# Head norm of the last mixer: the four tiles of squares are added on VectorE before one product with ones

## The chip, the cores and the metric

One core of one Trainium2 chip runs the whole program. The metric is the device time of one execution in microseconds, as the median of three runs. A profile is one further execution; its times are read from its trace.

## The reference

Two transformer blocks run over 256 tokens of width 2048, in fp32. The first has three attention branches and a convolutional feed-forward part. The second has an attention mixer over 272 tokens (16 of them meta tokens) and then a gated linear attention (GLA) mixer. The change lies in the end of the GLA mixer:

```
o = (o_f + o_b).transpose(0, 2, 1, 3)[:, pad:]            # per token: 4 heads x 512 values
o = rmsnorm_2(o, o_norm).reshape(B, L, GLA_VALUE_DIM)     # x * rsqrt(mean(x*x) + eps) * w, over the 512 values of a head
return (o * jax.nn.silu(g_out[:, pad:])) @ w_out
```

## The kernel before

**Weights.** Every weight matrix is streamed in units of 128x1024 fp32 (two k tiles by 512 columns). SyncE loads a unit into `raw`, ScalarE copies it to `whi` (rounded for a fast product, L655) and VectorE makes the rest `wlo = raw - whi` (L1304). TensorE multiplies each unit in three passes, (whi, ahi), (whi, alo), (wlo, ahi): 24 products of 128x256 a unit in the stage of this case (L2078). `whi` and `wlo` are rings of four units; ScalarE and VectorE work `LEAD = 3` units ahead of TensorE. ScalarE may start the split of unit u+3 only when TensorE has finished unit u-1 (`ring_waits`).

**The stage `gg`.** The gate projection of the GLA mixer is 4 trips of 8 units, its outputs go through Silu to `gg`. Beside these units, each engine runs the GLA of the four heads. Head h begins at unit `HEAD_AT[h] = 8 * h`, and `head_step(h, lag)` says what an engine does for head h at `lag` units after that. Each engine has its own program in which a step's order is written out by hand:

- TensorE: first the 24 products of the unit, then `head_step` of all heads.
- ScalarE and VectorE, in `trip`: first the split of the unit three ahead, then the read-out of finished banks (at the eighth unit of a trip), and then `head_step` of all heads.

**One head.** TensorE makes the scores at lag 0 and 1 (L2565, L2573), and the head's output of 512 values by 256 tokens at lag 3, in banks 6 and 7, as four tiles `v` of 128x256 (L2617, L2618; `o3_ready`). At lag 3 ScalarE squares them in two instructions into `osq3` (L1236; `o3_sq`) and loads the table of Sqrt (L700). At lag 4 TensorE multiplies the four tiles of squares with a 128x128 matrix of ones, into one bank, which sums over the 512 values and leaves the sum on all partitions (L2624; `o3_sum`); ScalarE takes the root (L1241; `o3_root`) and VectorE the reciprocal (L1978; `o3_rstd`). At lag 5 VectorE scales the four tiles, from the banks (L1982; `o3_scaled`). At unit 8h+7 (`GATED_AT`) VectorE multiplies with `gg` (L2005; `z3_ready`). The next head's scores wait for `o3_root` at its lag 0, and its far scores for `o3_scaled` at its lag 1. VectorE also has for the next head, at its lag -2 (lag 6 of this head), the products of L1950 and L1922.

**The rest.** Stage `gout` multiplies with `w_out`, reads the banks with `gainrow` (L2018), and the last residual is added. The DMA of `gainrow` is issued by ScalarE at lag 3 of the last head (L1232) and counted on its own semaphore `gain_in`. In the trace the tiles `osq3`, `gqk` and `v3` appear as `osq`, `gqk` and `v`.

Of the kernel before, what the change touches and what calls it, by code (L numbers as in the profile page):

```python
# [19 lines left out]
ALU = mybir.AluOpType  # L20
# [6 lines left out]
TB = 256  # L27
# [100 lines left out]
def two_blocks_kernel(nc, A, out):  # L128

    ctx = ExitStack()  # L130
    with ctx:
# [30 lines left out]
        ones = sb("ones", [P, P])  # L162
# [98 lines left out]
        gainrow = sb("gainrow", [P, D], F32, at_=R2 + KD * T2 * 4 + 4 * 2 * D)  # L261
# [4 lines left out]
        bank = ctx.enter_context(nc.psum_tensor("bank", [P, 8, 512], F32))  # L266
# [60 lines left out]
        def unit_source(ph, i, j):  # L327
# [70 lines left out]
        x_parked, x_back, up_clear, gla_const, z_sum, z_abs, z_min, z_exp, z_ln, z_sub, cum_ready, v3_turned, v3_taken = map(  # L398
            sem, "x_parked x_back up_clear gla_const z_sum z_abs z_min z_exp z_ln z_sub cum_ready v3_turned v3_taken".split())
# [2 lines left out]
                sem, "e_q e_k e_d e_dec d_sub q_dec k_inv k_end k_far sc_sum x_sum xm_sum sc_part sc_own sc_ready scm_ready "  # L402
                     "o3_ready o3_sq o3_sum o3_root o3_rstd o3_scaled z3_ready z3hi".split())

        gain_in, out_made, stored = map(sem, "gain_in out_made stored".split())


        LO, lo_tiles = {}, 0
# [236 lines left out]
        def _(act):  # L645
# [561 lines left out]
            def head_step(h, lag):  # L1207

                lf, lb = decays(h)
                if lag == -6:  # L1210
                    for d, t in enumerate((kendf, kendb)):
                        act.wait_ge(d_sub, 3 * h + 2 + d)
                        act.activation(t[:, :, :], t[:, :, :], ACT.Exp, scale=SC).then_inc(e_d, 1)
                    if h:
                        act.wait_ge(sc_sum, 2 * h)
                    for d, l in enumerate((lf, lb)):
                        act.activation(kinv[:, d, :, :], l[:, :, 0:TB], ACT.Exp, scale=-SC).then_inc(e_k, 1)
                if lag == -5:
                    if h:
                        act.wait_ge(x_sum, h)  # L1220
                    for d, l in enumerate((lf, lb)):
                        act.activation(qdec[:, d, :, :], l[:, :, 0:TB], ACT.Exp, scale=SC).then_inc(e_q, 1)
                    act.activation(dec[:, 0, :, :], lf[:, :, GL_CHUNK - 1:TB:GL_CHUNK], ACT.Exp, scale=SC).then_inc(e_dec, 1)
                    act.activation(dec[:, 1, :, :], lb[:, :, 0:TB:GL_CHUNK], ACT.Exp, scale=SC).then_inc(e_dec, 1)
                if lag == 1:
                    act.wait_ge(xm_sum, h + 1)
                    act.activation(scm[0:TM, :], bank[0:TM, 6, 0:TB], ACT.Copy)
                    act.activation(scm[32:32 + TM, :], bank[0:TM, 6, 0:TB], ACT.Copy).then_inc(scm_ready, 1)
                if lag == 3:
                    act.wait_ge(o3_ready, h + 1)  # L1230
                    if h == GL_HEADS - 1:
                        act.dma_start(gainrow[:, :], gain_all).then_inc(gain_in, 16)  # L1232
                    if h:
                        act.wait_ge(z3_ready, h)
                    for c in range(2):
                        act.activation(osq3[:, 2 * c:2 * c + 2, :], bank[:, 6 + c, :].rearrange("p (v t) -> p v t", v=2),  # L1236
                                       ACT.Square).then_inc(o3_sq, 1)
                    load_table(4 + 2 * h, ACT.Sqrt)
                if lag == 4:
                    act.wait_ge(o3_sum, h + 1)  # L1240
                    act.activation(msq[:, 0:TB], bank[:, 4, 0:TB], ACT.Sqrt, bias=eps, scale=1.0 / GL_V).then_inc(o3_root, 1)  # L1241
# [51 lines left out]
        def _(dve):  # L1293
# [649 lines left out]
            def head_step(h, lag):  # L1943

                if lag == -6:
                    to_ends(h)
                if lag == -2:
                    for d in range(2):
                        dve.wait_ge(e_q, 2 * h + d + 1)
                        dve.tensor_tensor(qdec[:, d, :, :], qdec[:, d, :, :], gqk[:, 2 * h:2 * h + 2, 0:TB], ALU.mult)\  # L1950
                           .then_inc(q_dec, 1)
                    far_keys(h)
                flat = sc[:, :, :].rearrange("p s t -> p (s t)")
                if lag == 0:
                    if h:
                        dve.wait_ge(o3_ready, h)
                    own = blocks(flat, 0, P, 0, TB + P, P)
                    other = tmp[:, 0, 0:TB].rearrange("p (t c) -> p t c", t=2)
                    for d, (dst, mask) in enumerate(((own, maskf), (other, maskb))):
                        dve.wait_ge(sc_sum, 2 * h + 2)  # L1960
                        dve.tensor_tensor(dst, bank[:, 4, d * TB:(d + 1) * TB].rearrange("p (t c) -> p t c", t=2),
                                          blocks(mask[:, :], 0, P, 0, 0, P), ALU.mult).then_inc(sc_part, 1)
                    dve.wait_ge(sc_part, 2 * h + 2)
                    dve.tensor_tensor(own, own, other, ALU.add).then_inc(sc_own, 1)
                if lag == 1:
                    dve.wait_ge(sc_own, h + 1)
                    dve.wait_ge(x_sum, h + 1)
                    dve.tensor_copy(flat[:, P:P + TB], bank[:, 5, 0:TB]).then_inc(sc_ready, 1)
                    dve.tensor_copy(blocks(flat, 0, 64, GL_CHUNK, TB + P, GL_CHUNK),
                                    bank[0:64, 5, TB:TB + P].rearrange("p (t c) -> p t c", t=2)).then_inc(sc_ready, 1)  # L1970
                    dve.tensor_copy(blocks(flat, 64, P, 0, TB + P, GL_CHUNK),
                                    bank[64:P, 5, TB:TB + P].rearrange("p (t c) -> p t c", t=2)).then_inc(sc_ready, 1)
                    dve.wait_ge(scm_ready, h + 1)
                    dve.tensor_tensor(scm[64:64 + TM, :], bank[0:TM, 6, 0:TB], scm[0:TM, :].bitcast(F32), ALU.subtract)\
                       .then_inc(scm_low, 1)
                if lag == 4:
                    dve.wait_ge(o3_root, h + 1)
                    dve.reciprocal(rstd[:, 0:TB], msq[:, 0:TB]).then_inc(o3_rstd, 1)  # L1978
                if lag == 5:
                    dve.wait_ge(o3_rstd, h + 1)  # L1980
                    for v in range(4):
                        dve.scalar_tensor_tensor(osq3[:, v, :], bank[:, 6 + v // 2, (v % 2) * TB:(v % 2 + 1) * TB],  # L1982
                                                 column("gla_o_norm_2", v), rstd[:, 0:TB], ALU.mult, ALU.mult)\
                           .then_inc(o3_scaled, 1)
# [25 lines left out]
            def rows_out(i, chunk, u, n):  # L2010

                if 2 * i + chunk == 0:
                    dve.wait_ge(gain_in, 16)
                for tt in range(2):

                    dve.wait_ge(y_squared, 24 + 2 * (2 * i + chunk) + tt + 1)
                    c = 512 * (2 * i + chunk)
                    dve.tensor_tensor(yrow[:, tt, c:c + 512], bank[:, 2 * chunk + tt, :], gainrow[:, c:c + 512], ALU.mult)\  # L2018
                       .then_inc(y_gained, 1)

            stream("gout", rows_out)

            for tt in range(2):
# [16 lines left out]
        def _(pe):  # L2040
# [561 lines left out]
            def head_step(h, lag):  # L2602

                if lag == 0:
                    scores(h)
                if lag == 1:
                    far_scores(h)
                if lag == 3:
                    pe.wait_ge(v3_taken, 3 * TRIPS["gv"])
                    pe.wait_ge(sc_ready, 3 * h + 3)  # L2610
                    pe.wait_ge(scm_low, h + 1)
                    pe.wait_ge(v_low, 2 + GL_HEADS)
                    for v in range(4):
                        col = h * GL_V + v * P
                        o = bank[:, 6 + v // 2, (v % 2) * TB:(v % 2 + 1) * TB]
                        for k in range(2):
                            pe.matmul(o, v3[:, k, col:col + P], sc[:, k, :], start=k == 0, stop=False)  # L2617
                        mm = pe.matmul(o, v3m[0:64 + TM, col:col + P], scm[0:64 + TM, :], start=False, stop=True)  # L2618
                    mm.then_inc(o3_ready, 1)
                if lag == 4:  # L2620
                    pe.wait_ge(sc_part, 2 * h + 2)
                    for v in range(4):
                        pe.wait_ge(o3_sq, 2 * h + v // 2 + 1)
                        mm = pe.matmul(bank[:, 4, 0:TB], ones[:, :], osq3[:, v, :], start=v == 0, stop=v == 3)  # L2624
                    mm.then_inc(o3_sum, 1)

            for i in range(TRIPS["gg"]):
                for j in range(UNITS["gg"]):
# [99 lines left out]
```

## Time and profile before

| | |
|---|---|
| median of 3 runs | 2286.8 us (2285.84 to 2286.86) |
| the profiled execution | 2286.57 us, its span 2284.8 us |
| TensorE busy | 2259.1 us, 99% |
| VectorE busy | 1435.2 us, 63% |
| ScalarE busy | 1172.5 us, 51% |
| stage `gg` | from about 2052 to 2186 us of the span |

The span is the time from the first to the last instruction in the trace; the execution's own time lies 1.8 us above it. TensorE's rows carry modelled ends: neighbouring products overlap on paper, so a unit's cost is read from the starts. A row of busy time by stretch gives the stretch and its length in us, the busy time (and number of instructions) of PE, PEld, DVE, ACT and POOL, the granted clock of TensorE, the DMA engines' share and GB/s.

### The profile page before, as it was taken

The page shows a single profiled execution, that of the slowest core. Times are in us where ns is not written, and L with a number is a line of the kernel's source. Part 1 is how long each engine was busy: PE and PEld are TensorE (multiplying, and loading weights), DVE is VectorE, ACT ScalarE, POOL GpSimd, SP SyncE. Part 2 cuts the span into 40 slices and gives each one's busy share as a digit, 9 for nine tenths or more (in the row PEclk, how much of TensorE's full clock was granted, in tenths as well). Part 3 has the DMA queues.
Part 4 walks back from the last instruction along what each step waited for, and adds up shares of the span by engine and source line. Part 5 has one row for each costly group of instructions (what it writes and reads, how often), then busy time and mean ns, then how long its engine had stood idle before and what let it go on. Part 6 is the DMA issues. An engine that isn't in the chain of part 4 may idle for free.

```text
span 2284.8 us, 43650 instructions
## 1 busy us (share of the span) xinstructions
PE 2259.1 (99%) x17147; PEld 2139.8 (94%) x17147; DVE 1435.2 (63%) x1843; ACT 1172.5 (51%) x1743; POOL 192.3 (8%) x146
## 2 busy tenths in 40 slices
PE   9999999999999999999999999999999999999998
PEld 9898999999899999999988889999999999999986
DVE  5556644458577777777744447997665464566654
ACT  5455544444454554554544445455555455675553
POOL 0000000000001222212200000221000000012110
PEclk9999999999999999999999999999999999999999
DMA  8545566656546656566665564555335556554453
GB/s 290 183 139 157 165 191 195 193 168 236 192 144 210 189 180 209 182 197 199 196 207 187 188 192 143 189 185 164 111 111 186 173 158 186 161 155 123 139 192 139
DMA packets 258873, 405.69 MB, mean 178 GB/s; under 512 B 16656, under 2 KB 115853, under 8 KB 257709
## 3 DMA queue, kind: packets, MB, share of 16 engines
q1 hardware_dynamic: 257060, 396.87, 55.2%
q10 hardware_dynamic: 1688, 7.07, 0.9%
q8 instruction: 89, 1.46, 0.3%
q14 instruction: 36, 0.29, 0.0%
HBM read 396.32 MB, written 4.22 MB: 175 GB/s over the span
## 4 chain that ended last, share of the span: by engine, by line
PE 95%; DVE 2%; ACT 2%; issue 0%; DMA 0%; ACTq 0%; DVEq 0%; SPq 0%
PE bank L2078 67%; PE bank L2183 14%; PE bank L2651 4%; PE bank L2093 2%; PE bank L2397 1%; PE bank L2432 1%; PE bank L2617 1%; PE bank L2573 1%; PE bank L2118 1%; ACT whi L655 0%; PE bank L2369 0%; DVE wlo L1304 0%; PE bank L2406 0%; DMA xtok<-in_x 0%; PE bank L2377 0%
## 5 line engine op out<-in xcount | busy, mean ns | idle before, releaser
L1304 DVE TENSOR_TENSOR wlo<-raw,whi 128x1024 fp32r<-128x1024 f32 (+1 forms) x748 | 927.9, 1250 | 697.3 <-ACT whi L655 694.0
L2078 PE MATMUL bank<-ahi,whi 128*128 128x256 f32 (+1 forms) x4224 | 1196.1, 283 | 3.4 <-DVE alo L1490 1.3
L2078 PE MATMUL bank<-ahi,wlo 128*128 128x256 f32 (+1 forms) x4224 | 1181.4, 280 | 0.0
L2078 PE MATMUL bank<-alo,whi 128*128 128x256 f32 (+1 forms) x4224 | 1181.4, 280 | 0.0
L655 ACT ACTIVATE whi<-raw 128x1024 fp32r<-128x1024 f32 (+1 forms) x748 | 774.7, 1040 | 714.7 <-PE bank L2078 476.8
L2078 PEld LDWEIGHTS bank<-ahi,whi 128*128 128x128 f32 x4224 | 794.2, 188 | 10.7 <-issue 5.3
L2078 PEld LDWEIGHTS bank<-alo,whi 128*128 128x128 f32 x4224 | 794.3, 188 | 1.4 <-issue 0.2
L2078 PEld LDWEIGHTS bank<-ahi,wlo 128*128 128x128 f32 x4224 | 794.4, 188 | 0.0
L2183 PE MATMUL bank<-whi,ghi 128*128 128x512 f32 x352 | 137.0, 389 | 0.0
L2183 PE MATMUL bank<-whi,glo 128*128 128x512 f32 x352 | 136.9, 389 | 0.0
L2183 PE MATMUL bank<-wlo,ghi 128*128 128x512 f32 x352 | 136.9, 389 | 0.0
L2669 POOL CAST ghi<-pr 128x256 f32 x44 | 40.0, 909 | 753.1 <-DVE pr L1701 753.1
L1694 DVE SCALAR_TENSOR_TENSOR cv<-bank,par,cv 128x255 f32<-128x255 f32 (+1 forms) x176 | 78.7, 478 | 11.9 <-DVE cv L1694 1.5
L2183 PEld LDWEIGHTS bank<-wlo,ghi 128*128 128x128 f32 x352 | 66.1, 188 | 13.8
L2183 PEld LDWEIGHTS bank<-whi,glo 128*128 128x128 f32 x352 | 66.1, 188 | 13.7
L2183 PEld LDWEIGHTS bank<-whi,ghi 128*128 128x128 f32 x352 | 66.1, 188 | 13.7 <-DVE wlo L1304 0.2
L2662 POOL TENSOR_TENSOR glo<-pr,ghi 128x256 f32 x44 | 65.8, 1494 | 7.2 <-POOL ghi L2669 7.2
L993 ACT ACTIVATE cv<-bank,par 128x256 f32<-128x256 f32 x88 | 42.5, 564 | 38.4 <-DVE bank L1688 38.4
L2078 PE MATMUL bank<-yhi,wlo 128*128 128x256 f32 x192 | 53.0, 276 | 0.0
L2078 PE MATMUL bank<-yhi,whi 128*128 128x256 f32 x192 | 53.0, 276 | 0.0
L2078 PE MATMUL bank<-ylo,whi 128*128 128x256 f32 x192 | 53.0, 276 | 0.0
L2679 POOL TENSOR_TENSOR nc<-n,cos 128x272 f32<-128x272 f32 x24 | 40.5, 1687 | 120.7 <-DVE n L1722 120.7
(357 smaller groups left out, 2192.8 us busy)
## 6 DMA issues: line engine op xcount, KB each, us to landing
raw<-in_w_up SPq DMA_DIRECT2D x176, 512.0 KB, 4.7
raw<-in_w_in SPq DMA_DIRECT2D x156, 512.0 KB, 4.2
raw<-in_attn_w_in SPq DMA_DIRECT2D x96, 512.0 KB, 4.1
raw<-in_gla_w_in SPq DMA_DIRECT2D x96, 512.0 KB, 3.7
raw<-in_w_down SPq DMA_DIRECT2D x80, 512.0 KB, 4.3
raw<-in_w_out SPq DMA_DIRECT2D x32, 512.0 KB, 4.5
raw<-in_attn_w_out SPq DMA_DIRECT2D x32, 512.0 KB, 3.7
raw<-in_gla_w_out SPq DMA_DIRECT2D x32, 512.0 KB, 4.2
```

The source lines that it names most:

```text
L655: act.activation(whi[:, u % RING, 0:c], raw[:, u % RAW, 0:c], ACT.Copy).then_inc(whi_ready, 1)
L993: act.activation(cv[:, t, :], bank[:, 4 * chunk + t, 0:TB], ACT.Identity, bias=par[:, bass.ds(i * 4 + (PAR["conv_b"] + r), 1)], scale=par[ ...
L1304: dve.tensor_tensor(wlo[:, u % RING, 0:c], raw[:, u % RAW, 0:c], whi[:, u % RING, 0:c].bitcast(F32), ALU.subtract).then_inc(wlo_ready, 1)
L1694: dve.scalar_tensor_tensor(cv[:, t, back:TB], bank[:, 4 * chunk + t, 0:TB - back], tap, cv[:, t, back:TB], ALU.mult, ALU.add).then_inc((ta ...
L2078: mm = pe.matmul(bank[:, base + t, 0:T], w[wp][:, k, col:col + P], rhs(ap, k0 + k), start=begins and k == 0 and (wp, ap) == (0, 0), stop=e ...
L2093: mm = pe.matmul(bank[:, first_bank + tt, 0:cols[1] - cols[0]], ha((ahi, alo)[ap], k0 + k, tt * P, P), w[wp][:, k, cols[0]:cols[1]], start ...
L2118: mm = pe.transpose(turned(k)[:, tt * P:(tt + 1) * P], src[:, tt, k * P:(k + 1) * P], ident[:, :])
L2183: mm = pe.matmul(bank[:, row_bank(b, c, tt), :], tokens_of, w[wp][:, k, :], start=begins and k == 0 and (wp, ap) == (0, 0), stop=ends and ...
L2651: mm = pe.matmul(bank[:, b, :], gated(ap, k0 + k)[:, tt * P:(tt + 1) * P], w[wp][:, k, :], start=begins and k == 0 and (wp, ap) == (0, 0), ...
L2662: pool.tensor_tensor(dst, whole, high.bitcast(F32), ALU.subtract).then_inc(done, 1)
L2669: pool.tensor_copy(ghi[:, bass.ds(i * 4 + t, 1), :], pr[:, t % 2:t % 2 + 1, :]).then_inc(ffhi_ready, 1)
L2679: pool.tensor_tensor(nc2[:, n % 2, :], n2[:, n % 2, :], cos[:, :], ALU.mult).then_inc(qk_cos, 1)
```

## The change

VectorE gets two additions at lag 4, in place in `osq3`: tiles 2 and 3 onto tiles 0 and 1 (128x512), and then tile 1 onto tile 0 (128x256). TensorE then makes one product with the ones where it made four. It waits for the second addition (`o3_added`) where it waited for ScalarE's squares (`o3_sq`). VectorE's reciprocal goes from lag 4 to lag 5, and its four scalings from lag 5 to lag 6. The semaphore `gain_in` goes: the DMA of `gainrow` counts on `gla_const`, which stands at 80 by then and reaches 96.

```
 # ScalarE, head_step, lag 3
                     if h == GL_HEADS - 1:
-                        act.dma_start(gainrow[:, :], gain_all).then_inc(gain_in, 16)
+                        act.dma_start(gainrow[:, :], gain_all).then_inc(gla_const, 16)
 # VectorE, head_step
                 if lag == 4:
+                    dve.wait_ge(o3_sq, 2 * h + 2)
+                    dve.tensor_tensor(osq3[:, 0:2, :], osq3[:, 0:2, :], osq3[:, 2:4, :], ALU.add).then_inc(o3_added, 1)
+                    dve.wait_ge(o3_added, 2 * h + 1)
+                    dve.tensor_tensor(osq3[:, 0, :], osq3[:, 0, :], osq3[:, 1, :], ALU.add).then_inc(o3_added, 1)
+                if lag == 5:
                     dve.wait_ge(o3_root, h + 1)
                     dve.reciprocal(rstd[:, 0:TB], msq[:, 0:TB]).then_inc(o3_rstd, 1)
-                if lag == 5:
+                if lag == 6:
                     dve.wait_ge(o3_rstd, h + 1)
                     for v in range(4):
                         dve.scalar_tensor_tensor(osq3[:, v, :], bank[:, 6 + v // 2, (v % 2) * TB:(v % 2 + 1) * TB],
 # VectorE, rows_out
-                    dve.wait_ge(gain_in, 16)
+                    dve.wait_ge(gla_const, 96)
 # TensorE, head_step
                 if lag == 4:
                     pe.wait_ge(sc_part, 2 * h + 2)
-                    for v in range(4):
-                        pe.wait_ge(o3_sq, 2 * h + v // 2 + 1)
-                        mm = pe.matmul(bank[:, 4, 0:TB], ones[:, :], osq3[:, v, :], start=v == 0, stop=v == 3)
-                    mm.then_inc(o3_sum, 1)
+                    pe.wait_ge(o3_added, 2 * h + 2)
+                    pe.matmul(bank[:, 4, 0:TB], ones[:, :], osq3[:, 0, :], start=True, stop=True).then_inc(o3_sum, 1)
```

## Rows read from the trace of the kernel before

**Rows 1.** The page, its part 1: each engine's busy time, share, instructions.

```profile
PE 2259.1 (99%) x17147; PEld 2139.8 (94%) x17147; DVE 1435.2 (63%) x1843; ACT 1172.5 (51%) x1743; POOL 192.3 (8%) x146
```

**Rows 2.** The page, its part 4: the chain that ended last, by engine.

```profile
PE 95%; DVE 2%; ACT 2%; issue 0%; DMA 0%; ACTq 0%; DVEq 0%; SPq 0%
```

**Rows 3.** Busy time by stretch: one head's eight units.

```profile
2087.30:2120.50 33.20, 33.20 (x294) 32.13 (x294) 20.64 (x35) 20.50 (x32) 8.51 (x5) 1.00 0.42 127
```

**Rows 4.** Timeline of TensorE (start us, length us) at lag 4 of heads 0 and 3.

```profile
2076.20 0.28 PE L2078 MATMUL bank<-ahi,wlo 128*128 128x256 f32 x1
2076.32 1.89 PE L2624 MATMUL bank<-osq,ones 128*128 128x256 f32 x8
2077.86 0.47 PE L2078 MATMUL bank<-ahi,whi 128*128 128x256 f32 x1
...
2175.91 1.89 PE L2624 MATMUL bank<-osq,ones 128*128 128x256 f32 x8
2177.46 0.47 PE L2078 MATMUL bank<-ahi,whi 128*128 128x256 f32 x1
```

**Rows 5.** Timeline of ScalarE, head 0, from its lag 3 to lag 5.

```profile
2073.77 1.09 ACT L1236 ACTIVATE osq<-bank 128x512 f32<-128x512 f32 x2 [1.66 <-PE bank L2618]
2074.88 1.28 ACT L700 ACT_TABLE_LOAD   x1
...
2076.28 1.04 ACT L655 ACTIVATE whi<-raw 128x1024 fp32r<-128x1024 f32 x1
2078.24 0.48 ACT L1241 ACTIVATE msq<-bank,lam 128x256 f32<-128x256 f32 x1 [0.92 <-PE bank L2624]
2078.62 1.05 ACT L655 ACTIVATE whi<-raw 128x1024 fp32r<-128x1024 f32 x1
```

**Rows 6.** Timeline of VectorE at lag 4 of heads 0 and 3.

```profile
2077.35 1.23 DVE L1304 TENSOR_TENSOR wlo<-raw,whi 128x1024 fp32r<-128x1024 f32 x1 [5.24 <-ACT whi L655]
2078.75 1.75 DVE L1978 RECIPROCAL rstd<-msq 128x256 f32<-128x256 f32 x1 [0.17 <-ACT msq L1241]
...
2177.35 1.22 DVE L1304 TENSOR_TENSOR wlo<-raw,whi 128x1024 fp32r<-128x1024 f32 x1 [8.26 <-ACT whi L655]
2178.49 1.74 DVE L1978 RECIPROCAL rstd<-msq 128x256 f32<-128x256 f32 x1
```

**Rows 7.** Lines L1908 and L1964 alone: shortest/median/longest ns.

```profile
L1908 DVE TENSOR_TENSOR kendf<-cum x4: 685/685/685, 2034.4 to 2133.2; 128x512 f32<-128x512 f32 x4
L1964 DVE TENSOR_TENSOR sc<-sc,tmp x4: 426/426/854, 2060.8 to 2158.6; 128x256 f32<-128x256 f32 x4
```

**Rows 8.** Timeline of GpSimd around heads 0 and 1.

```profile
2070.92 3.58 POOL L2695 TENSOR_TENSOR kinv<-kinv,gqk 128x512 f32<-128x512 f32 x2
2090.38 2.39 POOL L2662 TENSOR_TENSOR z0lo<-gg,z0hi 128x1024 fp32r<-128x1024 f32 x1 [15.88 <-ACT z0hi L1263]
```

**Rows 9.** The chain in order of time, where TensorE resumes in an earlier stage.

```profile
1845.88 0.04 issue
1845.93 3.50 PE bank L2118 x16
...
1852.30 0.44 PE bank L2118 x4
```

**Rows 10.** Busy time by stretch, there and around L2212's waits; columns as in group 3.

```profile
1842.80:1846.10 3.30, 0.79 (x8) 0.60 (x7) 2.73 (x7) 1.81 (x6) 0.00 (x0) 1.00 0.00 0
1846.20:1849.60 3.40, 3.40 (x18) 3.40 (x17) 1.89 (x6) 2.66 (x7) 0.00 (x0) 0.50 0.00 0
...
1880.30:1890.60 10.30, 8.59 (x75) 8.40 (x75) 6.35 (x9) 3.92 (x6) 0.00 (x0) 1.00 0.86 291
```

**Rows 11.** TensorE's waits, whole span: total us, times, longest us.

```profile
PE bank L2212 <- DVE mstat L1530: 3.2, 2, 1.7
PE bank L2118 <- DVE xn L1483: 3.1, 2, 2.5
```

**Rows 12.** Timeline of VectorE at lag 0 of head 1.

```profile
2091.40 0.42 DVE L1961 TENSOR_TENSOR sc<-bank,maskf 128x256 f32<-128x256 f32 x1 [1.06 <-PE bank L2565]
```

More of the change, by code:

```diff
@@ L403, in two_blocks_kernel @@
                      "o3_ready o3_sq o3_sum o3_root o3_rstd o3_scaled z3_ready z3hi".split())
-        gain_in, out_made, stored = map(sem, "gain_in out_made stored".split())
+        o3_added, out_made, stored = map(sem, "o3_added out_made stored".split())
         LO, lo_tiles = {}, 0
```

## The prediction

> **What bounds the kernel now.** I read the page first: TensorE is busy 99% of the span [rows 1] and holds 95% of the chain that ended last [rows 2]. The reader should take from this that a microsecond taken from TensorE's program is a microsecond of time, and that a microsecond of waiting put into it is one lost, as long as nothing else is late. Then the busy time by stretch: eight units of one head take 33.2 us in which TensorE has no idle time at all at a full clock, while VectorE works 20.6 us and ScalarE 20.5 us [rows 3]. So the stage of the change has room on the engine that gets work and none on the one that loses it. That share is an average, though. What matters is whether VectorE has the two additions ready at the moment at which TensorE asks for them, and that is read from the timelines of the three engines at lag 4.
>
> **TensorE, what is removed.** The four products with ones stand in the trace as eight records, from 2076.32 to the start of the next unit at 2077.86: 1.54 us for a head [rows 4]. One product in place of four costs a quarter, 0.39 us, so 1.15 us goes for each head and 4.6 us for four. At head 3 the stretch is 1.55 us [rows 4]; heads 1 and 2 repeat head 0 33.2 us apart. Were the sums ready in time, that would be all.
>
> **VectorE, when the sums are ready.** Today the squares are what TensorE waits for. ScalarE starts them at 2073.77 and goes on to the table at 2074.88, over a microsecond before TensorE's last product of the unit at 2076.20, so this wait is free [rows 4, 5]. In the changed kernel the additions stand in VectorE's program behind the split of the same step. That split starts at 2077.35, after VectorE has sat idle for 5.24 us, waiting for ScalarE's `whi` [rows 6]. ScalarE in turn makes that `whi` only at 2076.28, because it has squares and the table load ahead of it in its own program [rows 5]. Nothing in the change touches this order, so the split keeps its time, and the additions come behind it:
>
> - split from 2077.35; the next instruction can start 1.14 us later (head 3: 2177.35 to 2178.49 [rows 6]): 2078.49.
> - first addition, 128x512, all in SBUF: 0.69 us, as L1908 [rows 7], and 0.03 us for the wait of the second on the first, which I estimate from the 0.04 us that TensorE needs after VectorE [rows 9]: 2079.21.
> - second addition, 128x256: 0.43 us, as L1964 [rows 7]: 2079.64.
> - TensorE resumes 0.04 us behind [rows 9]: 2079.68. One product: 0.39 us. The next unit begins at 2080.07, against 2077.86.
>
> That is 2.21 us later for a head; the trace repeats the same distances at heads 1 and 2, each 33.2 us on. At head 3 the split starts at 2177.35 and the next unit began at 2177.46 [rows 4, 6]: the same steps end at 2180.07, so the loss is 2.61 us. Sum: 3 x 2.21 + 2.61 = 9.2 us. From start to start TensorE stands 3.36 us (2076.32 to 2079.68) and gets back 1.15 us of it; by modelled ends (2076.20 + 0.28) the trace would show 3.2 us of idle time, and 3.6 us at head 3.
>
> The additions are priced from neighbours, so both ends: a chain of instructions that don't wait for each other starts 0.08 us sooner, and 0.1 us less each for a head gives 8.8 us; the longest of the L1964 rows took 0.85 us, twice the usual. GpSimd was working on 128x1024 at that time (2090.38 to 2092.77), whereas around lag 4 it had finished at 2074.50 [rows 7, 8]. I therefore take the short value; with the long one 0.43 us more for each head gives 10.9 us.
>
> **Can the wait be paid back?** Only by idle time of TensorE behind it, and there is none in the stage [rows 3]. It stays.
>
> A rule of the Trainium skill bears on the order: the page "TensorE: Matmul & The Clock Gate", section "Architectural detail: the array is 16× 32×32, not 1× 128×128", says that ScalarE's and VectorE's queues are strict FIFO. By it the additions can't use the 5.24 us of idle time ahead of the split, and the sum is a loss of 9.2 us; could they overtake, it would be a gain of 4.6 us. The trace agrees so far: the reciprocal stands behind the split at each head.
>
> **The clock.** TensorE's clock is full in this stage [rows 3]. Earlier in the trace there is one wait of 2.5 us, the longest of all [rows 11], with TensorE busy only 0.79 us in 3.3 us, and the granted clock right after it is 0.50 (1.2 GHz) for 3.4 us [rows 10]. The waits of up to 1.7 us at L2212 [rows 11] brought none: the clock there is 1.00 [rows 10]. The new waits of 3.2 us are longer than the one that brought it. Price of one fall: 16 turns took 3.50 us there, and at a full clock four took 0.44 us, so 16 take 1.76 us [rows 9]: 1.7 us lost; that also is half of 3.4 us. Part of a low stretch can lie in the wait itself, so I take 1.6 us. One example can't say that every such wait brings a fall, as the one before was followed and preceded by thinner work; I take three of four: 4.8 us. Ends: none and all four at 1.7, 0 to 6.8 us.
>
> The same page of the Trainium skill, section "HAM oscillation — how this bites in real kernels", describes such waits between groups of products as what throttles the clock each time. By it all four would fall: 6.4 us in place of 4.8.
>
> **The moved steps.** Root, reciprocal and scalings come later. ScalarE's root started 0.38 us after the next unit's first product (2077.86 to 2078.24), its next split 0.38 us after that [rows 4, 5]: now 2080.45 and 2080.83, so VectorE's split of lag 5 starts at 2081.9. From there VectorE has the same work as it had from the reciprocal at 2078.75 until it fell idle 1.06 us before 2091.40 [rows 6, 12]: 11.6 us, only in another order, the scalings behind the next head's L1950 and L1922. It ends at 2093.5, and the scores that it then waits for come 2.21 us later than before, at 2093.6. So VectorE has just caught up by the next head; the far scores, which wait for the scalings, come a unit after that. Splits are three units ahead, and none of these comes more than about a unit later. I price this at nothing; without the cover it would be a part of a unit's wait for a head. In head 3 no next head's work stands in between, and `gg`'s last read-outs hold the gating anyway.
>
> **The semaphore.** `gainrow`'s DMA keeps its queue and place and is used a whole stage later, whichever count tells of it: nothing.
>
> **Sum.** 2286.8 + 9.2 + 4.8 = 2300.8 us. The profiled execution was 2286.57 us with a span of 2284.8; a profile after would show a span near 2298.8. The median lies 0.2 us above that execution, which changes nothing.
>
> **The rivals.**
>
> - *The wait without the clock.* The stretches around the new waits are dense, unlike the one in the old trace; the clock may not fall, or once. 2286.8 + 9.2 = 2296.0, with one fall 2297.6. For it: the single example. Against: the waits are longer than that one's.
> - *The additions are ready in time.* TensorE doesn't wait, and the removed products are the whole effect: 2286.8 - 4.6 = 2282.2 us, faster. This needs the second addition done by 2076.2 in place of 2079.64, so that the split does not stand ahead of it or its `whi` comes 3.5 us sooner; below a delay of 1.15 us behind 2076.32 the change gains. Only the program's written order speaks against it, but that order shows in each head: split, then reciprocal [rows 6].
> - *It comes out even.* The additions would have to end near 2077.5, so that wait and saving cancel: 2286.8. No row puts VectorE there, since even its split ends after that.
> - *More is late.* The 0.1 us of margin at the next head goes, or GpSimd slows the additions, or the clock stays low for longer than one stretch: 10.9 + 6.8 = 17.7 us and more, 2304.5 and up.
>
> **How the numbers follow.** The wait with two falls or more (2299.2 to 2302.4; forecast 2300.8): 0.55. The wait with one or none: 0.30. More is late: 0.08. Additions in time: 0.04. Even: 0.03. The three runs before spread over 1.0 us, so about 0.2% (4.6 us) can be told from nothing. Slower by over 0.2%: 0.93, within: 0.03, faster: 0.04. The range reaches from the low end of the wait without a fall, 2286.8 + 8.8 = 2295.6 less half a microsecond of spread, 2295.0, to just short of both upper ends together (10.9 + 6.8: 2304.5), 2304.0; what lies outside is the 0.15 of the last three cases. The likeliest case's own range is 2298.8 (8.8 and two falls) to 2302.8 (9.2 and four falls at 1.7).
>
> **What would show it.** In the timeline of TensorE at lag 4, two records of L2624 in place of eight, with an idle time of about 3.2 us before them, ended by VectorE's `osq`, four times; in VectorE's, the split at the same distance behind the unit as before, and two additions of 0.69 and 0.43 us directly behind it; granted clock 0.50 in a stretch of 3.4 us behind some of the waits; no new waits of L2565, L2573 or L2617. The prediction is wrong if the additions stand ahead of the split or overlap the unit, if the clock stays at 1.00 behind all four waits (then 2296), or if a second wait appears at lag 0 or 1 of the next head.

## The result

The changed kernel takes 2298.18 us (median of 5, 2296.67 to 2301.49) against 2286.67 us before (median of 5): 11.5 us longer, ratio 1.0054 with an interval of 1.0041 to 1.0067. The forecast was 2300.8 us with a range of 2295.0 to 2304.0. The profiled execution took 2298.08 us with a span of 2296.3 us, where before had 2284.8.

TensorE's waits over the whole span of the changed kernel, longest in total first (who waited for whom, us in total, times, longest us):

```profile
PE bank L2628 <- DVE osq L1980: 13.6, 4, 3.7
PE bank L2123 <- DVE xn L1483: 3.1, 2, 2.5
PE bank L2217 <- DVE mstat L1530: 2.5, 2, 1.5
```

The first row is new: at each of the four heads L2628, the one product with ones, waits for L1980, the second addition. The two others answer to [rows 11].

ScalarE at lag 3 to 5 of head 0 in the changed kernel (timeline: start us, length us, idle time before it and what ended it):

```profile
2073.60 1.09 ACT L1236 ACTIVATE osq<-bank 128x512 f32<-128x512 f32 x2 [1.66 <-PE bank L2623]
2074.71 1.28 ACT L700 ACT_TABLE_LOAD   x1
...
2076.11 1.04 ACT L655 ACTIVATE whi<-raw 128x1024 fp32r<-128x1024 f32 x1
2080.32 0.47 ACT L1241 ACTIVATE msq<-bank,lam 128x256 f32<-128x256 f32 x1 [3.17 <-PE bank L2628]
2080.69 1.05 ACT L655 ACTIVATE whi<-raw 128x1024 fp32r<-128x1024 f32 x1
```

VectorE in the same stretch, and at lag 0 of head 1:

```profile
2077.18 1.23 DVE L1304 TENSOR_TENSOR wlo<-raw,whi 128x1024 fp32r<-128x1024 f32 x1 [5.24 <-ACT whi L655]
2078.32 0.68 DVE L1978 TENSOR_TENSOR osq<-osq 128x512 f32<-128x512 f32 x1
2079.04 0.42 DVE L1980 TENSOR_TENSOR osq<-osq 128x256 f32<-128x256 f32 x1
...
2093.28 0.42 DVE L1961 TENSOR_TENSOR sc<-bank,maskf 128x256 f32<-128x256 f32 x1
```

TensorE at lag 4 of heads 0 and 3:

```profile
2076.03 0.28 PE L2083 MATMUL bank<-ahi,wlo 128*128 128x256 f32 x1
2079.61 0.67 PE L2628 MATMUL bank<-osq,ones 128*128 128x256 f32 x2 [3.31 <-DVE osq L1980]
2079.93 0.47 PE L2083 MATMUL bank<-ahi,whi 128*128 128x256 f32 x1
...
2187.35 1.19 PE L2628 MATMUL bank<-osq,ones 128*128 128x256 f32 x2 [3.71 <-DVE osq L1980]
2187.99 0.78 PE L2083 MATMUL bank<-ahi,whi 128*128 128x256 f32 x1
2188.56 0.42 PE L2083 MATMUL bank<-alo,whi 128*128 128x256 f32 x1
```

Read them against [rows 4 to 6]. VectorE still sits idle for 5.24 us until ScalarE has made `whi`; it then makes the split, and only then adds. The sums exist at 2079.46 (2079.04 + 0.42), and TensorE resumes at 2079.61. From its last product of the unit (2076.03) to the first of the next (2079.93) it now needs 3.90 us, where it needed 1.66 us: 2.24 us lost at head 0. At head 3 the idle time is 3.71 us, and the two records behind it are 1.19 us long instead of 0.67: the clock is low there, as the stretches below show. The last row of VectorE has no idle time before it; [rows 12] had 1.06 us.

Busy time of the changed kernel by stretch: the wait of head 0 and what follows it, the same for head 1, and what follows the wait of head 3 (columns as in [rows 3]; the value before the last two is the granted clock):

```profile
2076.30:2079.60 3.30, 0.00 (x1) 0.02 (x1) 2.25 (x3) 0.85 (x1) 0.00 (x0) 1.00 0.00 1
2079.60:2083.00 3.40, 3.39 (x28) 3.35 (x29) 1.22 (x2) 1.42 (x2) 0.00 (x0) 1.00 0.55 154
...
2112.10:2115.40 3.30, 0.65 (x4) 0.63 (x5) 2.25 (x3) 0.18 (x1) 0.00 (x0) 1.00 0.19 16
2115.50:2118.90 3.40, 3.40 (x19) 3.40 (x18) 1.99 (x2) 1.38 (x2) 0.00 (x0) 0.52 0.38 139
...
2187.20:2190.60 3.40, 3.25 (x13) 3.10 (x14) 0.57 (x2) 1.42 (x2) 0.00 (x0) 0.52 0.45 157
```

The waits of heads 0 and 1 have the same length (3.31 us of idle time); behind head 0's the clock stays at 1.00, behind head 1's it is 0.52. I call such a stretch of low clock a fall. In this execution there was one at heads 1 and 3, and none at heads 0 and 2.

The chain in order of time then shows what a fall costs in the 96 products behind L2628, for heads 0 to 2:

```profile
2079.61 0.67 PE bank L2628 x2
2080.28 10.89 PE bank L2083 x96
...
2114.75 0.67 PE bank L2628 x2
2115.42 12.51 PE bank L2083 x96
...
2151.50 0.67 PE bank L2628 x2
2152.17 11.31 PE bank L2083 x96
```

Head 1 with a fall takes 1.6 us longer than head 0 without one. Head 2, also without one, takes 11.31 us. That second difference of 0.42 us is not the granted clock, which is 1.00 behind both; it comes back below as TensorE's pace.

### The profile page after: what moved, and what is told of

It reads as the page before. It is cut to its first block, busy times and chain, and to the rows that moved or that the text cites. A ratio compares the mean times of both kernels' runs of the same rounds, so it can differ in the third digit from the quotient of the medians.

```text
span 2296.3 us, 43610 instructions
## 1 busy us (share of the span) xinstructions
PE 2258.2 (98%) x17123; PEld 2139.0 (93%) x17123; DVE 1440.0 (63%) x1851; ACT 1172.2 (51%) x1743; POOL 192.3 (8%) x146
## 4 chain that ended last, share of the span: by engine, by line
PE 94%; DVE 3%; ACT 2%; issue 1%; DMA 0%; ACTq 0%; DVEq 0%; SPq 0%
PE bank L2083 66%; PE bank L2188 14%; PE bank L2654 4%; PE bank L2098 2%; PE bank L2402 1%; PE bank L2437 1%; ACT whi L655 1%; PE bank L2622 1%; DVE wlo L1304 1%; PE bank L2578 1%; PE bank L2123 1%; PE bank L2374 0%; PE bank L2411 0%; PE bank L2382 0%; DMA xtok<-in_x 0%
## 5 line engine op out<-in xcount | busy, mean ns | idle before, releaser
L2188 PEld LDWEIGHTS bank<-whi,ghi 128*128 128x128 f32 x352 | 66.1, 188 | 13.7 <-DVE wlo L1304 0.2
L2188 PEld LDWEIGHTS bank<-whi,glo 128*128 128x128 f32 x352 | 66.1, 188 | 13.7
```

What stands on the lines that cost most here:

```text
L2188: mm = pe.matmul(bank[:, row_bank(b, c, tt), :], tokens_of, w[wp][:, k, :], start=begins and k == 0 and (wp, ap) == (0, 0), stop=ends and ...
```

## The experiments

My theory: the additions stand behind a split that waits for ScalarE; TensorE waits for them; some of the waits bring the clock down; the moved reciprocal and scalings cost nothing. The rivals: the moved steps cost something (rival A in the expectations), the additions are slow wherever they stand (rival B), or the clock has no part in it. Each experiment is compared with the kernel before on the same chip. "Stage" below is the time in the chain from the first product behind head 0's scores to the first product of `gout`: before, the chain has these at 2058.09 and 2186.29, 128.20 us; in the changed kernel at 2057.93 and 2197.82, 139.89 us.

**The additions ahead of the split.** One change to the changed kernel: the two additions leave `head_step` and are made before the split of the same unit (shortened).

```
+            def add_squares(i, j):                      # at lag 4, run by trip ahead of the split
+                for h in range(GL_HEADS):
+                    if 8 * i + j == HEAD_AT[h] + 4:
+                        ... the two additions ...
-                trip("gg", i, after=gla)
+                trip("gg", i, before=add_squares, after=gla)
```

> The changed kernel, with VectorE's two additions ahead of the split of lag 4 instead of behind it; reciprocal and scalings stay a unit later. Theory (the additions stand behind a split that waits for ScalarE, and TensorE waits for them): they now run in VectorE's idle time from 2074.7 and end about 2075.8, before TensorE asks at about 2076.2, so no wait, no fall of the clock, and one product of 0.32 us where four took 1.54 us: 4 x 1.2 = 4.9 us less than before, about 2281.8 us. Rival A (the moved reciprocal and scalings cost part of it): the wait goes but the time stays above about 2284. Rival B (the additions themselves are too slow wherever they stand): TensorE still shows waits for the added tile, time 2286 or more.

Measured: 2279.34 us against 2285.97, ratio 0.9972 (0.9961 to 0.9982), 6.6 us less than before. VectorE, timeline:

```profile
2074.32 0.69 DVE L2011 TENSOR_TENSOR osq<-osq 128x512 f32<-128x512 f32 x1 [2.77 <-ACT osq L1236]
2075.05 0.42 DVE L2013 TENSOR_TENSOR osq<-osq 128x256 f32<-128x256 f32 x1
2076.78 2.54 DVE L1304 TENSOR_TENSOR wlo<-raw,whi 128x1024 fp32r<-128x1024 f32 x2 [1.31 <-ACT whi L655]
```

The additions use the idle time ahead of the split and are ready at 2075.47 (2075.05 + 0.42). The chain of this kernel around the ones:

```profile
2073.16 2.75 PE bank L2086 x24
2075.91 0.43 PE bank L2631 x2
2076.34 10.91 PE bank L2086 x96
```

TensorE's waits for the additions are gone; at head 3 alone it still stands 0.12 us before the ones, since the additions end only just in time there. So the place of the additions, with the wait and the falls that it brings, is all that was wrong with the change, and rivals A and B are ruled out. The gain is larger than the 4.9 us that I expected, though: the 96 products behind the ones take 10.91 us, where the chain before has 11.31. In the chain the stage shrinks by 6.0 us (from 128.20 to 122.18); the other 0.6 us of the difference of medians does not lie in it.

**The same with the old lags.** Reciprocal at lag 4 and scalings at lag 5 again:

```
-                if lag == 5:
+                if lag == 4:
                     dve.wait_ge(o3_root, h + 1)
...
-                if lag == 6:
+                if lag == 5:
                     dve.wait_ge(o3_rstd, h + 1)
```

> As the run with the additions ahead of the split, and reciprocal and scalings back at lag 4 and lag 5 as before the change. Theory (the moved steps cost nothing): the same as that run within 0.5 us, about 2281.8 us. Rival A (the moved steps cost): this one is faster than it by 1 us or more. A reciprocal at lag 4 that has to wait for the root would show as VectorE idle time of some tenths of a microsecond, on no path.

Measured: 2279.81 us against 2285.97, ratio 0.9974 (0.9964 to 0.9983). The two agree within 0.5 us: no effect of where the reciprocal and the scalings stand can be told from the spread.

**The moved steps alone**, on the kernel before:

```
-                if lag == 4:
+                if lag == 5:
                     dve.wait_ge(o3_root, h + 1)
...
-                if lag == 5:
+                if lag == 6:
                     dve.wait_ge(o3_rstd, h + 1)
```

> The kernel before, with nothing but the reciprocal at lag 5 and the scalings at lag 6; four products, no additions. Theory: no difference, 2286.7 us within 0.5. Rival A (the moved steps hold up the next head's scores or far scores): slower by 1 us or more, with a wait at L2573 or L2565.

Measured: 2286.13 us against 2285.97, ratio 1.0002 (0.9993 to 1.0011); the stage takes 128.20 us, as before to the hundredth, without a wait of TensorE.

**The wait without the saving.** The changed kernel with four products of the added tile:

```
-                    pe.matmul(bank[:, 4, 0:TB], ones[:, :], osq3[:, 0, :], start=True, stop=True).then_inc(o3_sum, 1)
+                    for v in range(4):
+                        mm = pe.matmul(bank[:, 4, 0:TB], ones[:, :], osq3[:, 0, :], start=v == 0, stop=v == 3)
+                    mm.then_inc(o3_sum, 1)
...
-                    act.activation(msq[:, 0:TB], ..., scale=1.0 / GL_V)
+                    act.activation(msq[:, 0:TB], ..., scale=0.25 / GL_V)
```

> The changed kernel, with four products of the added tile in place of one and the scale of the root a quarter, so the result is the same and the saving on TensorE is given up while the wait stays. Theory: TensorE's wait is as in the changed kernel and 4 x 1.2 us are added, about 2298.2 + 4.9 = 2303 us. Rival (the products lie beside something else that ends later, so their number is free): 2298 to 2299.

Measured: 2306.44 us against 2285.97, ratio 1.0089 (1.0075 to 1.0103): 20.5 us above before, some 9 us above the changed kernel's 11.5. The products are on the path, so the rival is ruled out; but I had expected 5 us. The waits are the same, 13.7 us in total. The profiled execution has the clock low for four stretches of 3.4 us in the stage, against two in the changed kernel's: one each at heads 2 and 3, and two in a row at head 1, where the clock was low from 1 us before TensorE resumed at 2116.93:

```profile
2115.90:2119.30 3.40, 2.37 (x6) 1.94 (x7) 0.85 (x2) 0.00 (x0) 0.00 (x0) 0.50 0.54 159
2119.30:2122.70 3.40, 3.40 (x15) 3.12 (x14) 0.53 (x1) 1.42 (x2) 0.00 (x0) 0.50 0.00 0
```

The pace behind eight records is the slower one at head 0 (11.31 us for 96 products). The additional falls and this pace are what I had left out.

**The wait filled.** The changed kernel with TensorE kept at work while it waits; the products' output is read by nobody:

```
+                    for _ in range(13):
+                        pe.matmul(bank[:, 4, TB:TB + P], ones[:, :], ident[:, :], start=True, stop=True)
                     pe.wait_ge(o3_added, 2 * h + 2)
```

> The changed kernel, with 13 products of 128x128 (ones by identity, into the free half of bank 4, read by nobody) in front of TensorE's wait at lag 4; by a row of the start of the kernel 7 such products take 1.73 us, so 13 take 3.2 us, which is the length of the wait. Theory (each fall of the clock costs about 1.6 us and comes from the idle time): the granted clock stays at 1.00 in the stage, the next unit starts when it did, and the time falls to about 2296 (before plus 9.2), with less spread than the changed kernel's 2296.7 to 2301.5. Rival (the clock's fall costs nothing, the rest is a late step): the time stays at 2298.

Measured: 2295.82 us (2293.63 to 2296.41) against 2286.87, ratio 1.004 (1.0026 to 1.0054). It lies where the theory had it, but the interval overlaps the changed kernel's, which had run on another chip. So both ran again on one chip.

> The changed kernel again, on the same chip as the filled one: 2298.2 us within 1.5, some 11.5 us above before.

> The filled wait again, beside the changed kernel on one chip. Theory (falls of the clock cost the changed kernel about 3 us): 2 to 3.5 us less than the changed kernel in the same call, no stretch of granted clock 0.50 in the stage. Rival (filling changes nothing): less than 1 us between the two.

Measured: changed 2300.2 us (2299.03 to 2300.66), ratio 1.0061 (1.0048 to 1.0075); filled 2295.15 us (2294.2 to 2296.32), ratio 1.004 (1.0026 to 1.0054); before 2286.26. The filled kernel is 5.05 us faster, and their times do not touch; I had expected 2 to 3.5. In this execution of the changed kernel the clock fell behind three of the four waits (heads 0, 2 and 3). Its chain at heads 0 and 1,

```profile
2079.64 12.51 PE bank L2083 x96
...
2116.39 11.31 PE bank L2083 x96
```

heads 2 and 3:

```profile
2151.84 12.51 PE bank L2083 x96
...
2188.98 9.79 PE bank L2083 x72
```

and the filled kernel's over the whole stage, by stretch, with a granted clock of 1.00:

```profile
2062.00:2196.00 134.00, 132.36 (x1184) 127.82 (x1182) 79.32 (x127) 71.73 (x110) 20.78 (x13) 1.00 0.44 130
```

In the filled kernel TensorE resumes no sooner (from the last product of the unit to the first of the next it takes 3.84 us at head 0, where the changed kernel takes 3.90), but the clock stays up: the falls are real time. Three of them at 1.6 us give 4.8 of the 5.05 us; the pace at head 1 (11.31 us here, 10.90 in the filled kernel) is of the size of the rest.

**A shorter wait.** The changed kernel with ScalarE's table load behind its split of lag 4:

```
-                    load_table(4 + 2 * h, ACT.Sqrt)
                 if lag == 4:
+                    load_table(4 + 2 * h, ACT.Sqrt)
```

> The changed kernel, with ScalarE's load of the table of Sqrt moved from lag 3, ahead of its split of lag 4, to lag 4, behind it. Theory (the additions wait for VectorE's split, that for ScalarE's): ScalarE's split, VectorE's split and the additions come 1.4 us sooner at each head, TensorE's wait falls from 3.3 to about 1.9 us, which is too short for a fall of the clock by the rows of before, so 2298.2 - 4 x 1.4 - 3 = about 2289.5 us. Rival (the additions wait for something else, for instance TensorE's own products or the squares): the wait stays at 3.3 us and the time at 2298.

Measured: 2290.51 us against 2286.87, ratio 1.0019 (1.001 to 1.0028). ScalarE's next steps and TensorE's waits:

```profile
2074.55 1.06 ACT L655 ACTIVATE whi<-raw 128x1024 fp32r<-128x1024 f32 x1
2075.63 1.28 ACT L700 ACT_TABLE_LOAD   x1
```

```profile
PE bank L2628 <- DVE osq L1980: 7.6, 4, 2.2
```

The wait falls from 13.6 to 7.6 us in total, 1.5 us a head, just by moving a step of ScalarE two links up the chain. One part went otherwise than expected: behind the longest wait, of 2.2 us at head 3, the clock fell all the same (2.5 us had been the shortest that I knew to bring it):

```profile
2180.50:2183.90 3.40, 3.40 (x19) 3.40 (x19) 2.06 (x2) 1.31 (x2) 0.00 (x0) 0.53 0.24 92
```

**Two products.** To test what the pace goes with: only the first of the two additions, ahead of the split, and two products. Against the kernel with both additions ahead:

```
-                        dve.wait_ge(o3_added, 2 * h + 1)
-                        dve.tensor_tensor(osq3[:, 0, :], osq3[:, 0, :], osq3[:, 1, :], ALU.add).then_inc(o3_added, 1)
...
-                    pe.wait_ge(o3_added, 2 * h + 2)
-                    pe.matmul(bank[:, 4, 0:TB], ones[:, :], osq3[:, 0, :], start=True, stop=True).then_inc(o3_sum, 1)
+                    pe.wait_ge(o3_added, h + 1)
+                    for v in range(2):
+                        mm = pe.matmul(bank[:, 4, 0:TB], ones[:, :], osq3[:, v, :], start=v == 0, stop=v == 1)
+                    mm.then_inc(o3_sum, 1)
```

> Additions ahead of the split, but only the first of them (128x512), and two products in place of one; reciprocal and scalings a unit later. Theory A (a saved product is worth its 0.39 us and nothing more): 2 x 0.39 x 4 = 3.1 us less than before, 2282.9 us. Theory B (fewer products also bring the next four units to the pace of 0.1134 us a product instead of 0.1178, 0.4 us a head): 4.7 us less, 2281.3 us, and the 96 products behind L2624's successor take 10.9 instead of 11.3 us.

Measured: 2281.51 us against 2286.26, ratio 0.9981 (0.9972 to 0.999). The chain:

```profile
2075.24 0.86 PE bank L2630 x4
2076.10 10.89 PE bank L2084 x96
```

4.75 us less than before, and the quicker pace: as theory B has it, at all four heads.

**All additions and all products.** Additions ahead of the split and four products of the added tile, with the edits shown above:

> Additions ahead of the split, and four products of the added tile with a quarter of the scale, so VectorE does all that the kernel with the additions first does and TensorE all that the kernel before does. Theory (the gain of the additions-first kernel lies in TensorE's products and the pace behind them): as before, 2286.0 us within 0.7. Rival (the additions or their place on VectorE bring part of the 6.6 us by themselves): 2284.5 us or less.

Measured: 2286.34 us against 2286.26, ratio 1.0 (0.9991 to 1.0009). The chain:

```profile
2075.29 1.73 PE bank L2632 x8
2077.02 11.31 PE bank L2086 x96
```

The additions by themselves are free and bring nothing, and behind eight records heads 0 to 2 have the slower pace again. All of the gain of the additions-first kernel is TensorE's.

The number of records isn't the whole cause of the pace, though. At head 3, with 72 products behind the ones, the kernel with the old lags has the slower pace behind two records (8.48 us), and this one the quicker behind eight (8.19 us):

```profile
2171.01 0.67 PE bank L2631 x2
2171.68 8.48 PE bank L2086 x72
```

```profile
2175.00 1.97 PE bank L2632 x8
2176.97 8.19 PE bank L2086 x72
```

TensorE stood 0.12 us before the ones in both.

## Why the prediction was right

**The wait.** The mechanism is the forecast one: the split kept its place, the additions took 0.68 and 0.42 us ([rows 7] gave 0.69 and 0.43), and a head lost 2.24 us (head 0) where 2.21 was forecast. That this agrees to 0.03 us is in part luck, since two small errors cancel: TensorE resumed 0.15 us behind the second addition, not 0.04, and the one product was cheaper than forecast. By the same starts, head 3 needed 2187.99 - 2183.36 = 4.63 us, where the last product's start is 3.71 us of idle time and 0.28 us before 2187.35; less 1.66 us and the 0.3 us that the low clock added between these starts, 2.7 us against 2.61. Sum 9.4 us for 9.2. What the rivals "ready in time" and "even" needed did not come; the first came when the additions were put ahead of the split by hand.

**One product's price** was that second error, a little too high: alone it takes 0.32 us from its start to the next unit, not the quarter of 1.54 us. So 1.22 us a head is saved, not 1.15.

**The clock.** The price of a fall (1.6 us) was measured at 1.6 us. The number was forecast as three, from a single example; it was two in the profiled execution and three in the later one, so that it came out near is partly luck. The rule that a page of the Trainium skill gives for such waits ("TensorE: Matmul & The Clock Gate", section "HAM oscillation — how this bites in real kernels") would have been four; no profile of the changed kernel shows four, and the waits of heads 0 to 2 are alike, so a wait's length alone doesn't decide. That the number changes between executions would make the times spread; the spread itself doesn't show it, with 4.8 and 1.6 us in the two sets of five against 1.0 to 3.4 us in the sets of the kernel before. Which wait brings a fall stays open.

**The moved steps** cost nothing, as forecast: VectorE just caught up (its 1.06 us of idle time at the next head went to nothing), and the run with these alone shows no difference (2286.13 us against 2285.97).

**What the sum left out** is the pace of TensorE behind the ones. In the changed kernel's profile it gives back 0.4 us at head 0, and none at head 2. The parts, for the profiled execution:

- the waits of heads 0 to 3, less the saved products: 9.4 us;
- the falls at heads 1 and 3: 1.6 us each (head 3: 1.19 us for the ones, which take 0.67 at full clock, and 9.27 us where 8.18 is the quick pace);
- given back by the pace: 1.0 us (0.42 less 0.09 in the unit behind the next scores at heads 0 and 1, and 0.30 at head 3).

That is 11.6 us, where the stage grew by 11.69 us. The later execution adds up in the same way: its stage grew by 13.29 us, and 9.4 us, three falls and 1.0 us given back make 13.2. The forecast of 14.0 us was high by one fall and this pace for the first execution, and mainly by the pace for the later one.

**The number alone** would not have told the cases apart. The median of 2298.18 us lies between the forecast's one fall (2297.6) and its two (2299.2), because the pace gave 1 us back; the range also held the rival without a fall, at 2296.0. It is the two falls in the trace and the filled wait that decide for the forecast case.

## What to carry to other kernels

Before work goes to an engine with idle time, look at where in its program the new instruction will stand, and what the instruction ahead of it waits for: VectorE was idle for 37% of the span, and this was no help, since the additions stood behind a split that waited for ScalarE, and the idle time at this point lay ahead of it. The same change costs 11.5 us with the additions behind that split and gains 6.6 us with them ahead of it. And when a full engine gets a wait of some microseconds, count its clock as well as the wait; if the wait can't be avoided, filling it with products that nobody reads gave back 5 us here.

## What the runs showed of the hardware

The same 96 products of 128x256 take 10.9 us or 11.3 us at a clock of 1.00 (0.1134 or 0.1178 us each). At heads 0 to 2, where nothing waited, the pace went with what stands ahead of them: eight records of ones gave 11.31 us (before, the moved steps alone, and all additions with all products), two or four gave 10.89 to 10.91 us. At head 3 this did not hold: the quicker pace came behind eight records once, and the slower behind two once. Behind a wait both occurred (10.89 and 11.31 us at heads 0 and 2 of the changed kernel). The traces show the step itself, not what causes it; that stays open. It is worth 0.42 us for four units, less 0.09 us in the unit behind the next scores: 0.33 of the 1.6 us that the additions-first kernel gained at each of heads 0 to 2.

Waits of 3.3 us brought the low clock behind some heads and not behind others of one execution, and one of 2.2 us brought it once, where the three waits of 1.8 us in the same execution did not. What one fall costs in this dense work is 1.6 us (12.51 us for 96 products at the quicker pace of 10.9).

TensorE resumed 0.14 to 0.15 us behind the end of the addition that it waited for (2187.21 to 2187.35 at head 3 of the changed kernel, 2079.46 to 2079.61 at head 0).
